# Scan of a two-block network: the mask product gives way to absolute value and exponential, and its scores move into the next half unit

## The reference, cut to what matters

```python
def segsum_decay(a_cs):
    q = a_cs.shape[-1]
    seg = a_cs[..., :, None] - a_cs[..., None, :]
    mask = jnp.tril(jnp.ones((q, q), dtype=bool))
    return jnp.exp(jnp.where(mask, seg, -jnp.inf))
...
    a_cs = jnp.cumsum(a, axis=-1)
    scores = jnp.einsum('bclgn,bcsgn->bgcls', cc, bc)
    mmat = scores[:, :, None] * segsum_decay(a_cs)
    y_diag = jnp.einsum('bghcls,bcsghp->bclghp', mmat, x)
    decay_states = jnp.exp(a_cs[..., -1:] - a_cs)
    states = jnp.einsum('bcsgn,bghcs,bcsghp->bcghpn', bc, decay_states, x)
    chunk_decay = jnp.exp(a_cs[..., -1])
```

## Time and profile before

| | us |
|---|---|
| median of 3 runs | 1715.36 (1715.27 to 1715.97) |
| the profiled execution | 1714.8 |
| its span in the trace | 1713.0 |
| PE busy, share of the span | 1658.9, 97% |
| DVE, ACT, POOL busy | 848.5, 667.8, 809.4 (50%, 39%, 47%) |
| share of PE in the chain that ended last | 84% |

### The profile page before, as it was taken

How to read it: one execution, slowest core, us unless ns; L and a number is a source line. 1 busy time by engine, 2 the same in 40 slices (tenths; PEclk the granted TensorE clock), 3 DMA queues, 4 the chain that set the end, 5 groups by cost and what they waited for, 6 DMA issues and landing times.

```text
span 1713.0 us, 22100 instructions
## 1 busy us (share of the span) xinstructions
PE 1658.9 (97%) x8138; PEld 1381.3 (81%) x8138; DVE 848.5 (50%) x1187; ACT 667.8 (39%) x1088; POOL 809.4 (47%) x670
## 2 busy tenths in 40 slices
PE   6999999999999999999999999989999999999997
PEld 5777788787878888888888889778878888888886
DVE  7546554556485445643235532677456654013324
ACT  3544434344223322543123322355656544234431
POOL 1364645545446555444444453333245554444444
PEclk7999999999999999999999999999999999999998
DMA  8121222122226445244555542121103142232221
GB/s 318 73 74 50 74 74 99 50 87 85 74 77 217 162 140 215 88 155 154 196 175 194 178 166 99 53 74 58 67 26 123 62 147 96 101 109 92 90 100 65
DMA packets 36826, 194.42 MB, mean 113 GB/s; under 512 B 4080, under 2 KB 6384, under 8 KB 21488
## 3 DMA queue, kind: packets, MB, share of 16 engines
q1 hardware_dynamic: 25200, 151.06, 24.4%
q10 hardware_dynamic: 11520, 41.95, 7.2%
HBM read 190.90 MB, written 2.10 MB: 113 GB/s over the span
## 4 chain that ended last, share of the span: by engine, by line
PE 84%; DVE 9%; ACT 3%; issue 2%; POOL 1%; DMA 0%; DVEq 0%; ACTq 0%; SPq 0%; POOLq 0%
PE main L901 62%; PE main L897 7%; PE main L894 2%; DVE tmp L2002 1%; PE auxB L1124 1%; PE auxD L1203 1%; PE main L999 1%; ACT w_hi L1427 1%; PE auxD L1268 1%; DVE ysum L2264 1%; PE auxC L1196 1%; PE auxB L1190 1%; DVE tmp L2558 1%; DVE ada_first L2170 0%; DVE x L2245 0%
## 5 line engine op out<-in xcount | busy, mean ns | idle before, releaser
L718 POOL TENSOR_TENSOR w_lo<-raw,w_hi 128x512 fp32r<-128x512 f32 x521 | 695.0, 1365 | 702.5 <-ACT w_hi L1427 698.8
L901 PE MATMUL main<-h_hi,w_hi 128*128 128x512 f32 (+1 forms) x1016 | 399.7, 393 | 0.0
L901 PE MATMUL main<-h_hi,w_lo 128*128 128x512 f32 (+1 forms) x1016 | 396.3, 390 | 0.0
L901 PE MATMUL main<-h_lo,w_hi 128*128 128x512 f32 (+1 forms) x1016 | 396.0, 390 | 0.0
L1427 ACT ACTIVATE w_hi<-raw 128x1024 fp32r<-128x1024 f32 (+2 forms) x267 | 257.7, 1013 | 249.9 <-PE main L901 178.2
L901 PEld LDWEIGHTS main<-h_hi,w_lo 128*128 128x128 f32 (+1 forms) x1016 | 190.5, 188 | 41.2 <-POOL w_lo L718 0.2
L901 PEld LDWEIGHTS main<-h_hi,w_hi 128*128 128x128 f32 (+1 forms) x1016 | 190.8, 188 | 39.9 <-issue 0.7
L901 PEld LDWEIGHTS main<-h_lo,w_hi 128*128 128x128 f32 (+1 forms) x1016 | 190.8, 188 | 39.6
L2145 DVE SCALAR_TENSOR_TENSOR tmp<-main,par,tmp 128x511 f32<-128x511 f32 x88 | 65.9, 749 | 165.6 <-ACT tmp L1539 164.0
L2170 DVE SCALAR_TENSOR_TENSOR ada_acc<-ada_raw,cs,ada_acc 128x1024 f32<-128x1024 f32 x70 | 106.7, 1525 | 35.0 <-DMA ada_raw<-w_ada 26.0
L897 PE MATMUL main<-w_hi,h_hi 128*128 128x512 f32 x224 | 90.7, 405 | 0.0
(11 more groups left out here) (525 smaller groups left out, 2849.8 us busy)
## 6 DMA issues: line engine op xcount, KB each, us to landing
raw<-stream SPq DMA_DIRECT2D x118, 1024.0 KB, 4.8
ada_raw<-w_ada ACTq DMA_DIRECT2D x80, 512.0 KB, 4.5
ada_first<-w_ada SPq DMA_DIRECT2D x16, 512.0 KB, 10.2
raw<-stream SPq DMA_DIRECT2D x8, 768.0 KB, 4.2
raw<-stream SPq DMA_DIRECT2D x8, 640.0 KB, 3.9
x<-x_in SPq DMA_DIRECT2D x4, 512.0 KB, 7.8
x<-x_in SPq DMA_DIRECT2D x1, 2048.0 KB, 9.2
out<-x SPq DMA_DIRECT2D x16, 128.0 KB, 1.8
```

What stands on the lines that cost most here:

```text
L718: nc.gpsimd.tensor_tensor(lo[:, a:b], raw[:, s, a:b], hi[:, a:b], ALU.subtract).then_inc(lo_done, 1)
L901: ins = nc.tensor.matmul(bank[0:n, :], w[:, k, col:col + n], a[:, ka_, :], start=start, stop=stop)
```

## The change

The mask product is gone. Without it the segment sums are positive at the masked places, so the exponential of minus their absolute value stays at most 1 there; the mask is multiplied into the 128 x 128 scores instead (`masked`, by the triangle `tri` of zeros and ones). ACT has three instructions per step instead of two (Abs of B, Abs of C, one exponential of 1024 columns with scale -1), and DVE one more of 128 columns, ahead of its wait for the exponential. `future_r` and `ident_r` are no longer made.

`ssd_scores` moves: from its slot after a half to a new table `early`, inside the half that follows. On PE it runs after 6 of that half's 24 matmuls, on ACT at the start of the half's part of the program (behind `split_hi` of the next unit and behind all steps of the slot before), on DVE ahead of the eviction of the half's last tile, on POOL ahead of `split_lo` for a first half, and behind the steps of `mid` for a second one. `ssd_out` keeps its slot, so it follows in the same half's end.

`seg_rows` and `seg_fill` move from the end of BC into the first half of Z0 (`inner`). PE's wait for `seg_fill` now asks for one chunk more at each of the first four steps.

```diff
-    end[find("BC")] += [("seg_rows", 0), ("seg_fill", 0)]
+    inner[find("Z0"), 0] += [("seg_rows", 0), ("seg_fill", 0)]
...
-            slot(scan + i).append(("ssd_scores", (g, i)))
+            early[(scan + i + 1) // 2, (scan + i + 1) % 2].append(("ssd_scores", (g, i)))
...
+                run(early[u.n, 0])
                 if u.n + 1 < len(units):
                     split_lo(units[u.n + 1])
                 run(inner[u.n, 0])
                 run(sorted(mid[u.n], key=xdt_first))
+                run(early[u.n, 1])
                 run(inner[u.n, 1])
...
+                if early[u.n, part]:
+                    within[jobs[0], 1] = lambda: run(early[u.n, part])
+                if inner[u.n, part]:
+                    within[jobs[1], 0] = lambda: run(inner[u.n, part])
...
-                if n == 0:
-                    pe.wait_ge(seg_set, 3)
+                if n < TC:
+                    pe.wait_ge(seg_set, 2 + n)
                 for b in range(2):
                     bank, full = take(("ssd_scores", i), 1 + b)
                     by_head = bank[:, :].rearrange("p (h t) -> p h t", h=4)
-                    nc.tensor.matmul(by_head, ident_r[:, :], each(future_r[:, :], 4), start=True, stop=False)
                     nc.tensor.matmul(by_head, seg_lhs[:, n % 2, :], seg_rhs[c][:, 4 * b:4 * b + 4, :],
-                                     start=False, stop=True).then_inc(full, 1)
+                                     start=True, stop=True).then_inc(full, 1)
...
-                    link(run_act(decay[:, 4 * b:4 * b + 4, :], bank[:, :].rearrange("p (h t) -> p h t", h=4), ACT.Exp))
+                    link(run_act(decay[:, 4 * b:4 * b + 4, :], bank[:, :].rearrange("p (h t) -> p h t", h=4), ACT.Abs))
                     act.sem_inc(free, 1)
-                act.sem_inc(seg_e, 1)
+                run_act(decay[:, :, :], decay[:, :, :], ACT.Exp, scale=-1.0).then_inc(seg_e, 1)
...
                     tiles = range(u.n_tiles // 2 * part_, u.n_tiles if part_ else u.n_tiles // 2)
+                    run(early[u.n, part_])
                     for t in tiles:
...
+                link(tt(masked[:, :], bank[:, 0:P], tri, ALU.mult))
+                dve.sem_inc(free, 1)
                 dve.wait_ge(seg_e, n + 1)
-                link(tt(decay[:, :, :], decay[:, :, :], each(bank[:, 0:P], HG), ALU.mult))
-                dve.sem_inc(free, 1)
+                link(tt(decay[:, :, :], decay[:, :, :], each(masked[:, :], HG), ALU.mult))
...
+                for part_, steps in ((0, mid), (1, end)):
+                    tiles = range(u.n_tiles // 2 * part_, u.n_tiles if part_ else u.n_tiles // 2)
+                    for t in tiles:
+                        if t == tiles[-1]:
+                            run(early[u.n, part_])
+                            run(inner[u.n, part_])
+                        if u.last:
+                            evict(u, t)
+                    run(steps[u.n])
```

More of the change, by code:

```diff
@@ L206, in plan_steps @@
     before, mid, end = ({u.n: [] for u in units} for _ in range(3))
-    inner = {(u.n, part): [] for u in units for part in range(2)}
+    early, inner = ({(u.n, part): [] for u in units for part in range(2)} for _ in range(2))
     at = {}
@@ L303, in plan_steps @@
     end[at["FD"][15]].append(("cross", 6))
-    order = [s for u in units for s in before[u.n] + inner[u.n, 0] + mid[u.n] + inner[u.n, 1] + end[u.n]] + last
-    return before, inner, mid, end, last, order
+    order = [s for u in units for s in before[u.n] + early[u.n, 0] + inner[u.n, 0] + mid[u.n]
+             + early[u.n, 1] + inner[u.n, 1] + end[u.n]] + last
+    return before, early, inner, mid, end, last, order
 BANKS_OF = {"ada_sum": "B", "dt_turn": "A", "dt_sums": "A", "seg_rows": "A", "b_turn": "A", "ssd_scores": "ABC",
@@ L340, in build @@
     units = plan_units()
-    before, inner, mid, end, last, order = plan_steps(units)
+    before, early, inner, mid, end, last, order = plan_steps(units)
     bank_use, used = {}, {b: 0 for b in "ABCD"}
@@ L1946, in _ @@
                     ACT.Tanh, scale=0.5).then_inc(cs_t, 1)
-            run_act(ident_r[:, :], ident, ACT.Copy)
             first_norm()
@@ L2773, in _ @@
                     continue
-                if u.last:
-                    for t in range(u.n_tiles // 2):
-                        evict(u, t)
-                run(inner[u.n, 0])
-                run(mid[u.n])
-                if u.last:
-                    for t in range(u.n_tiles // 2, u.n_tiles):
-                        evict(u, t)
-                run(inner[u.n, 1])
-                run(end[u.n])
+                for part_, steps in ((0, mid), (1, end)):
[7 more added lines that the diff above has]
+                    run(steps[u.n])
             run(last)
```

15 lines of the change are left out of this document (5 added, 10 removed).

## The result

The changed kernel takes 1744.56 us (median of 4 runs, 1742.67 to 1746.69) against 1715.66 of the kernel before (4 runs): 1.0167 times as long, 95% interval 1.0153 to 1.0182. It is slower by 28.9 us, where 20.1 were forecast.

The account below looks back on a forecast made before the run. PE was busy 97% of the span, but the loop through ACT and DVE was taken as longer than PE's half. 6.7 + 13.8 = 20.5 on 1714.8 gave 1735.3, predicted 1735.5 us, range 1721 to 1746.

Parts of the forecast that it names:

- The loop from one product to the next: Step (g, 2): DVE's passes, squares, split, scores and exponential return the product after 12.8 us; PE arrives at 9.9.
- Waits in groups 1 to 3: PE's waits for DVE's product: 1.15, 0.85, 2.9 and 1.7 us in blocks 0 to 3, 6.6 per group.
- rival 3: PE's waits of 0.85 to 2.9 us bring the lower clock, leaving 1 to 4 us per group: 1745; chance 0.12.
- Savings: PE without mask products, less added operand type changes: net 2.0 us saved per group, groups 1 to 3.
- Z0 and the segment rows: PE stands 6.2 us for bank A until 96.1, low clock on Z0's second half: +3.0 us, bounds +0.2 and +3.6.
- Group 0 with Z0: Z0's later end, group 0's steps and the low clock in its last half together: +6.7 us.
- the turn of `z`: Group 0, L1212 waits for bank D while DVE does X0's convolution and the passes of (0, 2): +0.2 us.
- Behind the scan: After the scan nothing differs except the shift.
- Rival 1: ACT and DVE answer before PE asks in every step: faster, 1696; chance 0.08 together with its half, 1705.

Follow-up runs that it names:

- math_only: The kernel before with only the new arithmetic (no mask products, absolute values, one exponential, masked scores), nothing moved: 1717.3 us, ratio 1.0003.
- scores_back: The changed kernel with the scores back in their old slots, new arithmetic and later segment rows kept: 1715.3 us, ratio 0.9992 to the kernel before.
- four_queues: The changed kernel with early scores put first on ACT, DVE and POOL, product operand in PSUM, segment rows back at BC's end: 1712.0 us, ratio 0.9976.
- psum_product: The changed kernel with masked scores written in place into bank A, so DVE's product has one operand in PSUM: 1735.1 us, ratio 1.0113 to the kernel before.
- fill_waits: The changed kernel with seven extra overwritten matmuls on PE ahead of the product wait in blocks 0 and 2 of each group: 1760.6 us, ratio 1.0268.
- fill_two: The changed kernel with two extra overwritten matmuls on PE ahead of the product wait in blocks 0 and 2 of each group: 1747.2 us, ratio 1.0186.

## Why the prediction was right, and where it was off

The direction and the mechanism held: removing work from the busiest engine made the kernel slower, because the early scores made new waits for the product (math_only and scores_back against the changed kernel show it; four_queues has the early scores and none of these waits, with the queues reordered, the product's operand in PSUM and the rows moved back). The loop from one product to the next is there: 13.1 us from the end of block (1, 1)'s product at 210.95 to that of block (1, 2)'s at 224.03, where 12.8 were forecast, and the wait that follows from it is 2.83 (0.91 + 1.92) where 2.9 was. The time lies in the range, 9 us above the forecast and 1.4 under the upper bound. That is in part luck: a cost of the clock that has no term is offset by terms that were too large. A slip in the last line is small: 1735.3 and 0.6 are 1735.9, not 1735.5. Term by term, on the profiled spans, 31.9 against 20.5, of which groups 1 to 3 are 22.5 against 13.8:

- **Waits in groups 1 to 3.** 6.6 a group forecast; 5.1, 4.5 and 4.8 measured, 5.5 less in all. Two mistakes partly cancel. The product was priced at 1.22 with its gaps to 1.4, from a row with an operand in PSUM; it is now SBUF with SBUF, and took 1.94 to 2.38 beside POOL's split. The prediction had met this in the earlier trace rows, in the pass that took 1.58 instead of 0.69 beside a POOL product, and didn't ask it of the new product. That made the wait of block 0 1.92 instead of 1.15 in group 1 (1.47 and 1.48 in groups 2 and 3). On the other side block 3's wait of 1.7 isn't there (0, 0.23 and 0) and block 1's is 0.34, 0 and 0.46 instead of 0.85: PE itself came late to them, at the low clock. Where neither happens (psum_product) my waits of blocks 0, 2 and 3 are 0.4 to 0.6 too long and that of block 1 right (0.82 for 0.85).
- **The clock, rival 3.** I gave it 0.12 and no term. By PE's busy time against psum_product it cost 4.6, 4.5 and 3.1 us in groups 1 to 3, 12 in all: the largest miss, and the term that failed. fill_waits shows the waits as its cause: with none over 0.90 us, no row of groups 1 to 3 is at the lower level. The forecast of 1745 under this rival is where the kernel came out, with its "1 to 4 us per group" somewhat low. The 12 us are of the profiled execution, the slowest of the four (granted clock 0.973 over the whole run, 0.976 to 0.978 in the others).
- **Savings.** 2.0 a group forecast. With no waits they are 2.2 (four_queues: 41.95 against 44.18), so the sum over blocks was right; among waits 44.18 - 42.85 = 1.3 is left of them, and in math_only 0.65. Where the rest of it goes among the waits of psum_product no run shows.
- **Z0 and the segment rows.** The wait for bank A is there as described: 5.97 us, ending at 95.55 where I had 6.2 and 96.1. The row of PE in the changed kernel, and the one for the rows themselves:

```profile
86.85 0.66 PE L1150 MATMUL auxA<-con,seg_left 128*128 128x128 f32 x4 [0.18 <-DVEq L2480]
...
95.55 1.12 PE L1167 MATMUL auxA<-con,bc 128*128 128x128 f32 x4 [5.97 <-DVEq L2490]
```

But the low clock that I let fall on the whole second half of Z0 (2.4 us) fell on part of it. The six products of 0.23 ahead of the scores at 104.45 put Z0's end at 103.1, 1.2 later than the earlier trace rows, 1.6 if the 0.4 us earlier start is counted, and not 3.0. The step that failed is the choice near the upper bound; the bounds, +0.2 and +3.6, held.
- **Group 0 with Z0.** 6.7 forecast, 5.3 measured: block (0, 3) comes at 151.53 and came at 146.25 (5.65 behind the turn of B, which starts 0.4 earlier). The parts: Z0 1.8 less than forecast; block (0, 0) 0.4 more and (0, 2), 13.1 from the one before instead of 12.55, 0.5 more, while (0, 1) is right (10.4 for 10.45); the turn of `z` right (+0.2, with a wait of 3.33 in it); the last half 0.5 less.
- **Behind the scan** I expected nothing, and 4.1 us are there in the profiled execution. They are hardly the change's: the same stretch took 1292.5 to 1298.7 us in the kernels of the experiments, 1292.8 in fill_waits, which has all of the change in it, and 1296.3 in math_only. The kernel after was profiled in its slowest run of four, and its median is 2.1 under it. What makes the stretch vary was not looked for.

**Rival 1** (the cover holds, 1696) was said to decide at a loop under 9.9 us, and fell. Of its 19 us four_queues, in which the loop no longer binds, got only 4: the waits of group 0 are still there.

**What the prediction didn't see** are the orders that decide whether the cover holds. It read DVE's tile ahead of the scores as a term of blocks 0 and 1 (0.7 us) and not as a crossing that makes the order on ACT work backwards. And it didn't see that `xdt` had lost its place ahead of the root on POOL: it says that the product would be the wait, which is true only as long as the queues of ACT and DVE are out of order.

## What to carry to other kernels

A step that runs over four engines is moved only when it has moved on all four: look, on each queue, at what now stands ahead of it, and at rules that sort it by name in the place it has left. Where two queues take the same two jobs in opposite order, whatever is put between them on one queue delays the other: a split of 2.0 us moved there cost 15 us, and nothing once the order was mended. And work in front of a wait is free up to the length of the wait it would uncover: before taking it from the busiest engine, look what that engine would wait for next.

## What the hardware showed that I had not expected

- A VectorE product of 1024 columns took 1.22 us in all 16 cases where one operand came from PSUM, and 1.22 to 2.38 with both in SBUF while GpSimd worked. Moving 128 columns to PSUM was worth 9 us of kernel time, and most of that through TensorE's clock, not through shorter standing (14.5 us in groups 1 to 3 against 14.3).
- Short waits can cost nearly as much again at the lower level of TensorE's clock: 5.1 us of standing in group 1 of the changed kernel came with 4.6 us more of busy time. With no wait over 0.90 us left (fill_waits) it was gone; with one of 1.74 us left (fill_two) it followed that one, and cost 1.6 and 3.1 us in the dense stretches behind.
